# A decoder layer with 32 experts: places of the weight ring, the last transfers in halves, and where the residual is added

## The chip, the cores and the metric

The kernel runs on one core of a Trainium2 chip. The metric is the device time of one execution in microseconds (us); the shown value is the median of three runs.

## The reference

One layer over 256 tokens of 1024 channels, all in fp32:

```
h = rms_norm(x, norm_mix)
x = x + token_mixer(h, ...)        # gated delta rule and mLSTM, 4 heads of 128 each
h = rms_norm(x, norm_ffn)
x = x + moe_ffn(h, ...)            # 32 experts, each token goes to 4 of them
return rms_norm(x, norm_final)

# in moe_ffn, for a token and each of its four experts e
gu   = h @ w_gate_up[e] + b_gate_up[e]            # 1024 -> 2048, gate and up interleaved
gate = min(gu[::2], 7);  up = clip(gu[1::2], -7, 7)
act  = gate * sigmoid(1.702 * gate) * (up + 1)
y    = act @ w_down[e] + b_down[e]                # 1024 -> 1024, weighted with the gate and summed
```

The weights of one expert are 8 MiB of w_gate_up and 4 MiB of w_down; all 32 experts are read, some 400 MB.

## The kernel before, in words

The mixer takes the first 315 us or so. It streams its weights in pieces of 1 MiB through eight half places of a ring in SBUF. The expert part follows and is the subject here.

**Items and groups.** An item is one expert with 64 token slots; a group is two items worked side by side, each on 64 columns of the PE array. There are 16 groups and one lone item (LONE). Group 8 (SHARED) is special: both of its items are the same expert, the one with the most tokens, so it needs one expert's weights for two items.

**The ring.** `ring` has ten places (DOUBLES) of 128 x 4096 fp32, 2 MiB each. An expert's weights are six tiles of that size: four gate/up tiles (GU, parts 0 to 3) and two down tiles (DN, sides 0 and 1). The list `doubles` (line 96 on) gives the order of the 192 transfers, and `released` the order in which PE is done with the tiles. In an ordinary group g both have GU of a, the four DN tiles of group g-1, GU of b. In group 8 `doubles` has the four GU tiles first and the DN tiles of group 7 behind them, while in `released` the DN tiles come first: PE uses the GU tiles twice (gate_up(8, 0) and gate_up(8, 1)) and lets go of them only in the second pass. Transfer i goes to place `ring_order[i % 10]`.

**SyncE (SP)** issues all these transfers on its queue in order. Before transfer i it waits until the tile that lay in this place, `doubles[i - 10]`, is released (`double_done`, line 399), and then calls `fetch` (line 355). `here` (line 300) is what PE waits for: the semaphore of the tile's place.

**PE**, per group n: gate_up(n, 0), down(n-1), gate_up(n, 1), transposes of the activations, scatter(n-1), gather of the rows for group n+1, transposes again. `scatter` (line 877) adds the expert outputs to the sums over all experts, which stay in PSUM banks 0 to 3 (two halves of 512 channels for each 128 tokens); `seed_sums` opens them with the bias of the down projection. At the end (from line 967) come gate_up of the lone item, down(15, side 0), its transposes, a wait for the copies of these by ACT and DVE, eight small products named keep_busy, down(15, side 1), the two sides of the lone item's down with the scatter of group 15 between them, and scatter_lone.

**DVE and ACT** do the clamped SwiGLU between gate_up and down, and the copies out of PSUM. At the end DVE adds the residual (`residual`, line 1381: four adds of 128x512, PSUM plus xs into xs), ACT squares xs and sums each row, DVE and ACT form the reciprocal root, and DVE multiplies xs with it and with norm_final into hn, which SP stores.

Of the kernel before, what the change touches and what calls it, by code (L numbers as in the profile page):

```python
# [20 lines left out]
F32 = mybir.dt.float32  # L21
# [4 lines left out]
ACT = mybir.ActivationFunctionType  # L26
AX = mybir.AxisListType

P = 128
# [5 lines left out]
HALF = 512  # L35
SLOTS = 64
RING = 8
DOUBLES = 10
MIXER_PLACES = 4
PIECE = 2048  # L40
# [3 lines left out]
def decoder_layer(nc, x, norm_mix, w_in, gdn_conv, gdn_a_log, gdn_dt_bias, gdn_norm, ml_conv,  # L44
# [71 lines left out]
    released.extend((DN, col, side) for side in range(2) for col in weights_of(N_GROUPS - 1))  # L116
    doubles.extend((DN, LONE, side) for side in range(2))
    released.extend((DN, LONE, side) for side in range(2))
    place_of = {d: i for i, d in enumerate(doubles)}
    release_of = {d: i for i, d in enumerate(released)}  # L120
    assert len(place_of) == len(release_of) == 6 * E

    with ExitStack() as ctx:
        def sb(name, shape, dt=F32):
# [4 lines left out]
        def sem(name):  # L129
            if name not in sems:  # L130
                sems[name] = ctx.enter_context(nc.semaphore(name))
            return sems[name]
# [120 lines left out]
        place = by_expert(MORE * EXTRA).rearrange("e (r k) -> e r k", r=MORE)  # L253
        placed, shift = by_expert(EXTRA), by_expert(EXTRA)

        bank = [ctx.enter_context(nc.psum_tensor(f"bank{i}", [P, HALF], F32)) for i in range(4)]
        bank45 = ctx.enter_context(nc.psum_tensor("bank45", [P, 2, HALF], F32))
        bank67 = ctx.enter_context(nc.psum_tensor("bank67", [P, 2, HALF], F32))
        B = [b[:, :] for b in bank] + [bank45[:, 0, :], bank45[:, 1, :], bank67[:, 0, :], bank67[:, 1, :]]


        onehot = ltm[:, 0, :, :]
# [21 lines left out]

        def double(d):

            return ring[:, ring_order[place_of[d] % DOUBLES], :]

        def full(place):

            if place < MIXER_PLACES:
                return f"w_full{2 * place}", MOE_FIRST // RING
            return f"ring_full{place}", 0

        def left_here(eng, place, n):

            name, before = full(place)
            eng.wait_ge(sem(name), n * 16 + 16 * (before + len([i for i in range(len(doubles)) if ring_order[i % DOUBLES] == place]) + 1))

        def here(eng, d):  # L300

            name, before = full(ring_order[place_of[d] % DOUBLES])
            eng.wait_ge(sem(name), 16 * (before + place_of[d] // DOUBLES + 1))

        def done_with(eng, d):

# [21 lines left out]
        def by_block(place, k):  # L328
            return place.rearrange("p (k c) -> p k c", k=k)
# [8 lines left out]
        def _(sp):  # L338
# [16 lines left out]
            def fetch(i, e):  # L355
                kind, col, part = doubles[i]
                src = (gu_v, dn_v)[kind][bass.ds(e, 1), :, part, :].rearrange("e p c -> p e c")
                sp.dma_start(by_block(double(doubles[i]), 1), src).then_inc(sem(full(ring_order[i % DOUBLES])[0]), 16)

            def fixed(col):  # L360
                return STAND_IN + 1 + col
# [28 lines left out]
                fetch(i, fixed(doubles[i][1]))  # L390

            expert = {col: fixed(col) for col in range(FIXED)}
            for i in range(DOUBLES, len(doubles)):
                col = doubles[i][1]
                if col not in expert:
                    if len(expert) == FIXED:
                        sp.wait_ge(sem("items_ready"), 1)
                    expert[col] = sp.value_load(ids[0:1, col:col + 1], min_val=0, max_val=E - 1)
                sp.wait_ge(sem("double_done"), release_of[doubles[i - DOUBLES]] + 1)
                fetch(i, expert[col])  # L400

            left = left_count(sp)
            with sp.If(left > 0):
# [73 lines left out]
        def _(pe):  # L477
# [354 lines left out]
            def down(n, sides=(0, 1)):  # L832

                if sides[0] == 0:
                    pe.wait_ge(sem("turned_copied"), n * 2 + 2)
                    pe.wait_ge(sem("xT_ready"), n * 2 + 4)
                for side in sides:
                    of = [(DN, weights_of(n)[min(e, len(weights_of(n)) - 1)], side) for e in range(2)]
                    for d in of:
                        here(pe, d)  # L840
                    for j in range(4):
                        at = j * P + side * SLOTS
                        for half in range(2):
                            for e in range(2):
                                mm = pe.matmul(B[6 + half][e * SLOTS:(e + 1) * SLOTS, :], actT[:, e, at:at + SLOTS],  # L845
                                               by_block(double(of[e]), 4)[:, j, half * HALF:(half + 1) * HALF],
                                               start=(side == 0 and j == 0), stop=(side == 1 and j == 3),
                                               skip_group_check=True)
                                if j == 3 and half == 1 and (e == 1 or of[0] != of[1]):
                                    mm.then_inc(sem("double_done"), 1)  # L850

            def down_lone(side, w):

                for j in range(4):
                    at = j * P + side * SLOTS
                    for half in range(2):
                        mm = pe.matmul(B[4 + half][half * SLOTS:(half + 1) * SLOTS, :], actT_left[:, at:at + SLOTS],  # L857
                                       by_block(w, 4)[:, j, half * HALF:(half + 1) * HALF],
                                       start=(side == 0 and j == 0), stop=(side == 1 and j == 3),
                                       skip_group_check=True)  # L860
                return mm
# [81 lines left out]
            turn_weighted(0, 1)  # L943
            open_gate_up(1, 0)
            turn_act(0, 1, 3)
            for n in range(1, N_GROUPS):
                gate_up(n, 0)
                pe.wait_ge(sem("scat_ready"), n)
                if n == 1:
                    seed_sums()  # L950
                down(n - 1)
                gate_up(n, 1)
                pe.wait_ge(sem("y_copied"), n * 2)
                turn_act(n, 0, 6)
                scatter(n - 1)
                pe.wait_ge(sem("onehot_ready"), n * (2 * T) + 4 * T)
                gather(n + 1, 1)
                pe.wait_ge(sem("turned_copied"), n * 2 + 1)
                gather(n + 1, 0)
                pe.wait_ge(sem("xT_ready"), n * 2 + 3)  # L960
                turn_act(n, 1, 7)
                pe.wait_ge(sem("xT_ready"), n * 2 + 4)
                turn_weighted(n, 6)
                open_gate_up(n + 1, 0)
# [4 lines left out]
            down(last, (0,))  # L969
            turn_act(N_GROUPS, 0, 4)  # L970
            turn_weighted(N_GROUPS, 5)
            pe.wait_ge(sem("turned_copied"), N_GROUPS * 2 + 1)
            pe.wait_ge(sem("scat_ready"), N_GROUPS + 1)
            keep_busy(8, 4)
            down(last, (1,))

            def scatter_lone():
                for t in range(T):
# [5 lines left out]

            for side in range(2):
                d = (DN, LONE, side)
                here(pe, d)
                down_lone(side, double(d)).then_inc(sem("double_done"), 1)
                if side == 0:
                    scatter(last)  # L990
            pe.wait_ge(sem("y_copied"), N_GROUPS * 2 + 2)
# [42 lines left out]
        def _(dve):  # L1034
# [607 lines left out]
                    dve.wait_ge(sem("sums_done"), n * T + 2 * T)  # L1642

            for t in range(T):
                dve.wait_ge(sem("sums_done"), t + 1)
                residual(t, "x3_ready")
            for t in range(T):
                mean_square(2, t)
            for t in range(T):
                dve.wait_ge(sem("root_ready"), 2 * T + t + 1)  # L1650
                link(dve.reciprocal(rstd[:, t:t + 1], rstd[:, t:t + 1]))
                dve.scalar_tensor_tensor(out=hn[:, t, :], in0=xs[:, t, :], scalar=rstd[:, t:t + 1], in1=fnorm[:, :],
                                         op0=ALU.mult, op1=ALU.mult).then_inc(sem("result_ready"), 1)


# [1 line left out]
        def _(se):  # L1657
# [174 lines left out]
            with se.If(left > 0):  # L1832
                with se.Fori(0, left) as n:
                    se.wait_ge(sem("glu_g_ready"), n + ITEMS + 1)
                    se.activation(glu_s, glu_g, ACT.Sigmoid, scale=SWIGLU_ALPHA).then_inc(sem("glu_s_ready"), 1)
                    se.wait_ge(sem("act_turned"), n + ITEMS + 1)
                    se.activation(actT_left, B[6], ACT.Identity).then_inc(sem("turned_copied"), 1)
                    se.wait_ge(sem("double_done"), n * 2 + len(doubles) + 2)
                    se.activation(ysb[0:SLOTS, 0:HALF], B[4][0:SLOTS, :], ACT.Identity).then_inc(sem("y_copied"), 1)
                    se.activation(ysb[SLOTS:P, HALF:D], B[5][SLOTS:P, :], ACT.Identity).then_inc(sem("y_copied"), 1)  # L1840
            se.activation(rstd[:, :], rstd[:, :], ACT.Sqrt).then_inc(sem("root_warmed"), 1)
            for t in range(T):
                se.wait_ge(sem("x3_ready"), t + 1)
                squares(t)
            for t in range(T):
                root(2, t)

# [21 lines left out]
```

## Time and profile before

| what | value |
|---|---|
| median of 3 runs | 1260.62 us (1257.66 to 1260.63) |
| profiled execution | 1257.48 us, its span 1255.5 us |
| PE busy | 1183.1 us, 94% |
| DVE, ACT, POOL busy | 314.8, 129.1, 33.7 us |
| moved by DMA | 441.27 MB, mean 351 GB/s over the span |
| mean granted TensorE clock | 0.985 |

The page divides the span in 40 slices of 31.4 us and gives for each the busy share of every engine and the GB/s of the transfers. A busy share says how much an engine does, not whether it sets the end. For that there are the waits (who waited for whom), the chain that ended last, and the time from the issue of a transfer to its landing, which holds the time in the queue behind earlier transfers too.

### The profile page before, as it was taken

How to read it: one execution, taken by the hardware profiler on the slowest of the kernel's cores; microseconds unless marked ns; L12 is line 12 of the kernel's file. 1: busy time of each engine (PE TensorE's matmuls, PEld its weight loads, DVE VectorE, ACT ScalarE, POOL GpSimd, SP SyncE). 2: the span in 40 equal slices, each digit the busy share in tenths (PEclk: the TensorE clock that was granted, in tenths of full speed). 3: DMA queues.
4: the chain of work that ended last, by engine and by line, in shares of the span. 5: the costliest groups of instructions: out<-in, count | busy, mean ns of one | idle time of the engine just before them, and what ended most of it. 6: DMA issues, size and time to landing. Idle time of an engine off the chain costs nothing.

```text
span 1255.5 us, 13834 instructions
## 1 busy us (share of the span) xinstructions
PE 1183.1 (94%) x5889; PEld 623.5 (50%) x5889; DVE 314.8 (25%) x686; ACT 129.1 (10%) x216; POOL 33.7 (3%) x48
## 2 busy tenths in 40 slices
PE   8999999999999999999899898999999898899986
PEld 6889999985633443434334242434434243434342
DVE  2784325252520211102011110102111010202012
ACT  3551001101000000000000000000000000000001
POOL 3700000000000000000000000000000000000000
PEclk9999999999899999999999999999999999999999
DMA  9933323474699999999999999899999999999993
GB/s 269 328 101 107 105 91 109 176 300 187 253 430 416 428 428 428 427 429 426 427 430 426 428 427 418 360 428 427 429 428 426 428 428 426 429 427 427 429 428 146
DMA packets 61582, 441.27 MB, mean 351 GB/s; under 512 B 8176, under 2 KB 32976, under 8 KB 36848
## 3 DMA queue, kind: packets, MB, share of 16 engines
q1 hardware_dynamic: 57104, 438.38, 85.0%
q10 hardware_dynamic: 4416, 1.99, 0.7%
q8 instruction: 48, 0.79, 0.3%
q14 instruction: 14, 0.11, 0.0%
HBM read 439.30 MB, written 1.05 MB: 351 GB/s over the span
## 4 chain that ended last, share of the span: by engine, by line
PE 65%; DMA 31%; DVE 3%; issue 0%; SPq 0%; ACT 0%; DVEq 0%
DMA ring<-in_w_down 31%; PE bank L805 21%; PE bank L845 14%; PE bank L493 13%; PE bank L509 3%; PE bank L785 3%; PE bank L746 2%; PE bank L882 2%; PE bank L716 1%; PE bank L705 1%; PE bank L797 1%; PE bank L857 1%; PE bank L516 1%; PE bank L579 0%; DVE cvg L1440 0%; PE bank L867 0%
## 5 line engine op out<-in xcount | busy, mean ns | idle before, releaser
L805 PE MATMUL bank<-ring,cvg 128*64 128x512 f32 x2112 | 461.6, 593 | 9.0 <-DMA ring<-in_w_gate_up 8.7
L805 PEld LDWEIGHTS bank<-ring,cvg 128*64 128x64 f32 x2112 | 151.2, 137 | 300.2 <-issue 274.9
L845 PE MATMUL bank<-ring,cvg 128*64 128x512 f32 x1024 | 236.3, 618 | 38.7 <-DMA ring<-in_w_down 38.7
L1450 DVE TENSOR_SCALAR cvm<-bank 128x512 f32<-128x512 f32 x33 | 22.8, 691 | 654.8 <-PE bank L805 654.8
L845 PEld LDWEIGHTS bank<-ring,cvg 128*64 128x64 f32 x1024 | 80.6, 142 | 192.5 <-issue 192.4
L493 PE MATMUL bank<-ring 128*128 128x256 f32 x768 | 171.7, 382 | 0.0
L493 PEld LDWEIGHTS bank<-ring 128*128 128x128 f32 x768 | 145.4, 192 | 19.9 <-issue 0.7
L1801 ACT ACTIVATE cvm<-cvm 128x512 f32<-128x512 f32 x33 | 20.8, 630 | 501.7 <-DVE cvm L1450 501.7
L785 PEld LDWEIGHTS bank<-ltm,hn 128*128 128x128 f32 x544 | 67.8, 199 | 7.1 <-issue 7.1
L785 PE MATMUL bank<-ltm,hn 128*128 128x128 f32 x544 | 67.9, 284 | 0.0
L882 PE MATMUL bank<-vb,ltm 128*128 128x512 f32 x128 | 57.7, 593 | 0.0
L1810 ACT ACTIVATE vb<-bank 128x512 f32<-128x512 f32 x32 | 17.4, 595 | 250.1 <-PE bank L845 250.1
L1440 DVE TENSOR_TENSOR cvg<-bank,ffn_rows 128x512 f32<-128x512 f32 x34 | 23.4, 691 | 66.2 <-PE bank L785 66.2
L882 PEld LDWEIGHTS bank<-vb,ltm 128*128 128x128 f32 x128 | 23.2, 192 | 23.8 <-issue 23.8
L1805 ACT ACTIVATE cvg<-bank 128x512 f32<-128x512 f32 x32 | 18.8, 588 | 99.2 <-PE bank L867 99.2
L746 PE MATMUL bank<-ring 128*128 128x512 f32 x64 | 27.6, 592 | 0.0
L867 PEld LDWEIGHTS bank<-ident,cvg 128*128 128x128 f32 x132 | 18.4, 206 | 13.4 <-issue 13.0
L1455 DVE SCALAR_TENSOR_TENSOR cvm<-cvm 128x512 f32<-128x512 f32 x33 | 22.9, 693 | 3.8 <-DVE cvm L1451 0.5
L1459 DVE TENSOR_TENSOR cvg<-cvm 128x512 f32<-128x512 f32 x33 | 22.8, 692 | 1.1
L867 PE MATMUL bank<-ident,cvg 128*128 128x128 f32 x132 | 22.9, 296 | 0.0
L1451 DVE TENSOR_SCALAR cvm<-bank 128x512 f32<-128x512 f32 x33 | 22.4, 680 | 0.0
L509 PEld LDWEIGHTS bank<-ring 128*128 128x128 f32 x176 | 20.6, 192 | 0.3
(315 smaller groups left out, 615.1 us busy)
## 6 DMA issues: line engine op xcount, KB each, us to landing
ring<-in_w_gate_up SPq DMA_DIRECT2D x128, 2048.0 KB, 34.6
ring<-in_w_down SPq DMA_DIRECT2D x64, 2048.0 KB, 36.7
ring<-in_w_in SPq DMA_DIRECT2D x24, 1024.0 KB, 6.6
ring<-in_w_out SPq DMA_DIRECT2D x4, 1024.0 KB, 5.0
ring<-in_w_up_ml SPq DMA_DIRECT2D x2, 1024.0 KB, 5.1
ring<-in_w_up_gdn SPq DMA_DIRECT2D x2, 1024.0 KB, 5.0
xs<-in_x SPq DMA_DIRECT2D x2, 512.0 KB, 4.6
out<-hn SPq DMA_DIRECT2D x2, 512.0 KB, 2.7
```

The source lines that it names most:

```text
L493: mm = pe.matmul(dst[:, c * S:(c + 1) * S], lhs, rhs, start=(k == 0), stop=(k == KC - 1))
L509: mm = pe.matmul(B[banks[i // 4]][:, (i % 4) * P:(i % 4 + 1) * P], lhs, rhs, start=True, stop=True)
L746: return pe.matmul(B[2 * t + n], gate_g[:, kk, t * P:(t + 1) * P], slot3((OUT_FIRST + i) % RING, 2)[:, k, n * HALF:(n + 1) * HALF], start= ...
L785: mm = pe.matmul(B[6 + b][:, (k % 4) * P:(k % 4 + 1) * P], by_row[:, k // 2, k % 2, :], onehot[:, t, :], start=(t == 0), stop=(t == T - 1))
L805: mm = pe.matmul(B[4 + half][side * SLOTS:(side + 1) * SLOTS, :], xT[:, k, e * SLOTS:(e + 1) * SLOTS], w[:, (k % 2) * PIECE + at:(k % 2) * ...
L845: mm = pe.matmul(B[6 + half][e * SLOTS:(e + 1) * SLOTS, :], actT[:, e, at:at + SLOTS], by_block(double(of[e]), 4)[:, j, half * HALF:(half ...
L867: mm = pe.transpose(B[to][:, c * P:(c + 1) * P], by_row[:, c, :], ident[:, :])
L882: mm = pe.matmul(B[2 * t + half], scat[:, t, :], ysb[:, half * HALF:(half + 1) * HALF], start=False, stop=False, skip_group_check=True)
L1440: dve.tensor_tensor(xT[:, 4 * b:4 * b + 4, :], B[6 + b].rearrange("p (k s) -> p k s", k=4), bc(ffn_rows[:, 4 * b:4 * b + 4].unsqueeze(2), ...
L1450: dve.tensor_scalar(g2, both[:, :, :, 0], SWIGLU_LIMIT, None, ALU.min).then_inc(sem("glu_g_ready"), 1)
L1455: dve.scalar_tensor_tensor(out=glu_u, in0=glu_u, scalar=1.0, in1=glu_g, op0=ALU.add, op1=ALU.mult).then_inc(sem("glu_u_ready"), 1)
L1459: dve.tensor_tensor(act[:, e, :], glu_u, glu_s, ALU.mult).then_inc(sem("act_ready"), 1)
```

## The change

1. *Places.* Transfer i goes to the place of `released[i - 10]` in place of `doubles[i - 10]`, and SP waits for that release. Up to group 8 both orders are the same.
2. *Halves.* The last six transfers, the four down tiles of group 15 and the two of the lone item, go out as two transfers of 1 MiB each with a semaphore for each half. The two tiles of a side alternate: first halves of both, then second halves. PE waits for the half that it needs.
3. *Order at the end.* down(15, side 1) moves ahead of the waits for the copies of the lone item's transposes, and keep_busy(8) goes.
4. *Residual.* In group 4 PE adds x (xs) into the sums by four products with the identity. DVE's adds at the end go. The last norm reads the sums from PSUM: ACT squares from there (into xs), and DVE's last product takes them from there.

```
-    place_of = {d: i for i, d in enumerate(doubles)}
-        bank = [... f"bank{i}", [P, HALF] ... for i in range(4)]
+        sums = [... f"bank{2 * t}{2 * t + 1}", [P, 2, HALF] ... for t in range(T)]

         def double(d):
-            return ring[:, ring_order[place_of[d] % DOUBLES], :]
+            return ring[:, place_at[d], :]
+        HALVED = doubles[-6:]
+        place_at, turn_at, turns = {}, {}, [0] * DOUBLES
+        for i, d in enumerate(doubles):
+            s = ring_order[i] if i < DOUBLES else place_at[released[i - DOUBLES]]
+            place_at[d], turn_at[d] = s, turns[s]
+            turns[s] += 1

+        def half_here(eng, d, half):
+            if half == 0:
+                here(eng, d)
+            else:
+                eng.wait_ge(sem(second_full(d)), 16 * (MOE_FIRST // RING + 1) if HALVED.index(d) < 4 else 16)

-            for i in range(DOUBLES, len(doubles)):
+            for i in range(DOUBLES, len(doubles) - len(HALVED)):
...
-                sp.wait_ge(sem("double_done"), release_of[doubles[i - DOUBLES]] + 1)
+                sp.wait_ge(sem("double_done"), i - DOUBLES + 1)
                 fetch(i, expert[col])
+            def fetch_half(d, half):
+                at = slice(half * PIECE, (half + 1) * PIECE)
+                src = dn_v[bass.ds(expert[d[1]], 1), :, d[2], at].rearrange("e p c -> p e c")
+                sp.dma_start(by_block(double(d)[:, at], 1), src).then_inc(...)
+            for pair in (HALVED[0:2], HALVED[2:4], HALVED[4:5], HALVED[5:6]):
+                sp.wait_ge(sem("double_done"), doubles.index(pair[-1]) - DOUBLES + 1)
+                for half in range(2):
+                    for d in pair:
+                        fetch_half(d, half)

@@ down
-                    for d in of:
-                        here(pe, d)
                     for j in range(4):
+                        for d in of:
+                            if d in HALVED:
+                                half_here(pe, d, j // 2)
+                            elif j == 0:
+                                here(pe, d)

+            def add_residual():
+                for t in range(T):
+                    for half in range(2):
+                        pe.matmul(B[2 * t + half], ident[:, :], xs[:, t, half * HALF:(half + 1) * HALF],
+                                  start=False, stop=False, skip_group_check=True)
             for n in range(1, N_GROUPS):
                 gate_up(n, 0)
...
+                if n == 4:
+                    add_residual()
                 down(n - 1)
@@ end of PE's work
             turn_weighted(N_GROUPS, 5)
+            down(last, (1,))
             pe.wait_ge(sem("turned_copied"), N_GROUPS * 2 + 1)
             pe.wait_ge(sem("scat_ready"), N_GROUPS + 1)
-            keep_busy(8, 4)
-            down(last, (1,))
...
-                here(pe, d)
-                down_lone(side, double(d)).then_inc(sem("double_done"), 1)
+                down_lone(side, double(d), lambda half: half_here(pe, d, half)).then_inc(sem("double_done"), 1)
@@ end of DVE's work
-                dve.wait_ge(sem("sums_done"), t + 1)
-                residual(t, "x3_ready")
...
-                dve.scalar_tensor_tensor(out=hn[:, t, :], in0=xs[:, t, :], scalar=rstd[:, t:t + 1], in1=fnorm[:, :],
+                dve.scalar_tensor_tensor(out=hn[:, t, :]..., in0=sums[t][:, :, :],
+                                         scalar=rstd[:, t:t + 1], in1=fnorm[:, :]...,
@@ end of ACT's work
-                se.wait_ge(sem("x3_ready"), t + 1)
-                squares(t)
+                se.wait_ge(sem("sums_done"), t + 1)
+                se.activation(xs[:, t, :]..., sums[t][:, :, :], ACT.Square,
+                              accum_out=ss[:, t:t + 1]).then_inc(sem("x_squared"), 1)
```

## Rows read from the trace of the kernel before

**Rows 1.** The page, its 40 slices: GB/s of all transfers in each.

```profile
GB/s 269 328 101 107 105 91 109 176 300 187 253 430 416 428 428 428 427 429 426 427 430 426 428 427 418 360 428 427 429 428 426 428 428 426 429 427 427 429 428 146
```

**Rows 2.** Windows: busy per engine (instructions), granted clock, DMA share, GB/s.

```profile
340.00:783.00 443.00, 417.56 (x2016) 169.72 (x2014) 76.77 (x191) 27.06 (x47) 0.00 (x0) 0.99 1.01 427
786.50:789.00 2.50, 2.50 (x14) 1.03 (x12) 0.00 (x0) 0.00 (x0) 0.00 (x0) 1.00 0.00 0
```

**Rows 3.** SyncE's issues from 1182 to 1190 us, and their time to landing.

```profile
L358 SPq DMA_DIRECT2D ring<-in_w_down x3: 332/333/333, 1182.3 to 1189.6; - x3
...
DMA to landing us min/median/max: 42.6/44.0/45.0
```

**Rows 4.** The chain that ended last, from 1166 us: start, us, what.

```profile
1166.31 8.59 PE bank L845 x32
...
1175.53 39.59 DMA ring<-in_w_down
...
1215.25 7.09 PE bank L845 x32
1222.33 0.68 PE bank L867 x4
...
1223.84 2.02 PE bank L524 x16
1225.86 7.02 PE bank L845 x32
1232.88 3.43 PE bank L857 x16
1236.31 3.63 PE bank L882 x8
1239.94 3.61 PE bank L857 x16
```

**Rows 5.** SyncE's issues from 741.5 to 789 us, two, and their time to landing.

```profile
L358 SPq DMA_DIRECT2D ring<-in_w_gate_up x2: 333/685/1037, 742.0 to 788.6; - x2
...
DMA to landing us min/median/max: 9.0/27.0/45.0
```

**Rows 6.** Timeline of PE around group 8: start, us, line, tiles, idle before.

```profile
767.67 7.09 PE L845 MATMUL bank<-ring,cvg 128*64 128x512 f32 x32 [2.44 <-DMA ring<-in_w_down]
777.46 7.09 PE L845 MATMUL bank<-ring,cvg 128*64 128x512 f32 x32 [2.70 <-DMA ring<-in_w_down]
...
784.78 13.93 PE L805 MATMUL bank<-ring,cvg 128*64 128x512 f32 x64
```

**Rows 7.** Time to landing: the issue at 863.3 us, then those from 520 to 560.

```profile
DMA to landing us min/median/max: 22.4/22.4/22.4
...
DMA to landing us min/median/max: 29.1/34.5/42.4
```

**Rows 8.** PE's waits from 784 to 1215 us: total, times, longest.

```profile
PE bank L845 <- DMA ring<-in_w_down: 17.2, 8, 2.7
```

**Rows 9.** Windows of 3.0 and 2.4 us, columns as in rows 2.

```profile
1166.30:1169.30 3.00, 2.99 (x8) 1.11 (x10) 0.00 (x0) 0.00 (x0) 0.00 (x0) 0.50 1.01 431
1212.80:1215.20 2.40, 0.03 (x2) 0.00 (x0) 2.18 (x4) 0.63 (x1) 0.00 (x0) 1.00 0.99 423
```

**Rows 10.** Timeline of DVE and ACT at the end.

```profile
1245.50 2.73 DVE L1386 TENSOR_TENSOR xs<-xs,bank 128x512 f32<-128x512 f32 x4 [1.23 <-PE bank L981]
1245.79 0.21 ACT L1841 ACTIVATE rstd<-rstd 128x8 f32<-128x8 f32 x1
1246.94 1.06 ACT L1664 ACTIVATE hn<-xs 128x1024 f32<-128x1024 f32 x1 [0.94 <-DVE xs L1386]
...
1248.27 1.06 ACT L1664 ACTIVATE hn<-xs 128x1024 f32<-128x1024 f32 x1 [0.17 <-DVE xs L1386]
...
1249.74 1.29 DVE L1652 SCALAR_TENSOR_TENSOR hn<-xs,rstd,fnorm 128x1024 f32<-128x1024 f32 x1
```

**Rows 11.** The page's costliest groups: ACT's copies out of PSUM.

```profile
L1810 ACT ACTIVATE vb<-bank 128x512 f32<-128x512 f32 x32 | 17.4, 595 | 250.1 <-PE bank L845 250.1
```

More of the change, by code:

```diff
@@ L118, in decoder_layer @@
     released.extend((DN, LONE, side) for side in range(2))
-    place_of = {d: i for i, d in enumerate(doubles)}
     release_of = {d: i for i, d in enumerate(released)}
-    assert len(place_of) == len(release_of) == 6 * E
+    assert len(set(doubles)) == len(release_of) == 6 * E
     with ExitStack() as ctx:
@@ L254, in decoder_layer @@
         placed, shift = by_expert(EXTRA), by_expert(EXTRA)
-        bank = [ctx.enter_context(nc.psum_tensor(f"bank{i}", [P, HALF], F32)) for i in range(4)]
+        sums = [ctx.enter_context(nc.psum_tensor(f"bank{2 * t}{2 * t + 1}", [P, 2, HALF], F32)) for t in range(T)]
         bank45 = ctx.enter_context(nc.psum_tensor("bank45", [P, 2, HALF], F32))
         bank67 = ctx.enter_context(nc.psum_tensor("bank67", [P, 2, HALF], F32))
-        B = [b[:, :] for b in bank] + [bank45[:, 0, :], bank45[:, 1, :], bank67[:, 0, :], bank67[:, 1, :]]
+        B = [sums[t][:, n, :] for t in range(T) for n in range(2)] + [bank45[:, 0, :], bank45[:, 1, :], bank67[:, 0, :], bank67[:, 1, :]]
         onehot = ltm[:, 0, :, :]
@@ L293, in full, with second_full @@
             return f"ring_full{place}", 0
+        def second_full(d):
+            i = HALVED.index(d)
+            return f"w_full{2 * i + 1}" if i < 4 else f"lone_full{i - 4}"
+        def half_here(eng, d, half):
[3 more added lines that the diff above has]
+                eng.wait_ge(sem(second_full(d)), 16 * (MOE_FIRST // RING + 1) if HALVED.index(d) < 4 else 16)
         def left_here(eng, place, n):
             name, before = full(place)
-            eng.wait_ge(sem(name), n * 16 + 16 * (before + len([i for i in range(len(doubles)) if ring_order[i % DOUBLES] == place]) + 1))
+            eng.wait_ge(sem(name), n * 16 + 16 * (before + turns[place] + 1))
         def here(eng, d):
-            name, before = full(ring_order[place_of[d] % DOUBLES])
-            eng.wait_ge(sem(name), 16 * (before + place_of[d] // DOUBLES + 1))
+            name, before = full(place_at[d])
+            eng.wait_ge(sem(name), 16 * (before + turn_at[d] + 1))
         def done_with(eng, d):
@@ L357, in fetch @@
                 src = (gu_v, dn_v)[kind][bass.ds(e, 1), :, part, :].rearrange("e p c -> p e c")
-                sp.dma_start(by_block(double(doubles[i]), 1), src).then_inc(sem(full(ring_order[i % DOUBLES])[0]), 16)
+                sp.dma_start(by_block(double(doubles[i]), 1), src).then_inc(sem(full(place_at[doubles[i]])[0]), 16)
             def fixed(col):
@@ L398, in _ @@
                     expert[col] = sp.value_load(ids[0:1, col:col + 1], min_val=0, max_val=E - 1)
[L399 removed]
+                sp.wait_ge(sem("double_done"), i - DOUBLES + 1)
                 fetch(i, expert[col])
+            def fetch_half(d, half):
+                at = slice(half * PIECE, (half + 1) * PIECE)
+                src = dn_v[bass.ds(expert[d[1]], 1), :, d[2], at].rearrange("e p c -> p e c")
+                sp.dma_start(by_block(double(d)[:, at], 1), src).then_inc(sem(second_full(d) if half else full(place_at[d])[0]), 16)
+            for pair in (HALVED[0:2], HALVED[2:4], HALVED[4:5], HALVED[5:6]):
[3 more added lines that the diff above has]
+                        fetch_half(d, half)
             left = left_count(sp)
@@ L850, in down, with down_lone @@
                                     mm.then_inc(sem("double_done"), 1)
-            def down_lone(side, w):
+            def down_lone(side, w, wait=None):
                 for j in range(4):
+                    if wait and j % 2 == 0:
+                        wait(j // 2)
                     at = j * P + side * SLOTS
@@ L1651, in _ @@
                 link(dve.reciprocal(rstd[:, t:t + 1], rstd[:, t:t + 1]))
-                dve.scalar_tensor_tensor(out=hn[:, t, :], in0=xs[:, t, :], scalar=rstd[:, t:t + 1], in1=fnorm[:, :],
+                dve.scalar_tensor_tensor(out=hn[:, t, :].rearrange("p (n c) -> p n c", n=2), in0=sums[t][:, :, :],
+                                         scalar=rstd[:, t:t + 1], in1=fnorm[:, :].rearrange("p (n c) -> p n c", n=2),
                                          op0=ALU.mult, op1=ALU.mult).then_inc(sem("result_ready"), 1)
@@ L1840, in _ @@
                     se.activation(ysb[SLOTS:P, HALF:D], B[5][SLOTS:P, :], ACT.Identity).then_inc(sem("y_copied"), 1)
+                    se.wait_ge(sem("sums_done"), n * T + 2 * T)
             se.activation(rstd[:, :], rstd[:, :], ACT.Sqrt).then_inc(sem("root_warmed"), 1)
             for t in range(T):
-                se.wait_ge(sem("x3_ready"), t + 1)
-                squares(t)
+                se.wait_ge(sem("sums_done"), t + 1)
+                se.activation(xs[:, t, :].rearrange("p (n c) -> p n c", n=2), sums[t][:, :, :], ACT.Square,
+                              accum_out=ss[:, t:t + 1]).then_inc(sem("x_squared"), 1)
             for t in range(T):
```

1 line of the change is left out of this document (removed).

## The prediction

> **What bounds the kernel now.** The page comes first: its 40 slices say which stretch has which limit. From slice 14 on the transfers move 426 to 430 GB/s, slice after slice, with dips in slices 25 and 26 alone (418, 360) until the last one [rows 1]. A stretch by itself confirms it: from 340 to 783 us the 16 DMA engines are busy 1.01 of the time at 427 GB/s [rows 2]. So the expert weights, 192 transfers of 2 MiB, set the pace. The chain of waits looks different, 65% PE, but its long DMA links (39.59 us for one transfer) are the time in the queue behind others, not the work of one.
>
> Two places are left where the transfers don't set the pace. One is the hole: at 786.5 to 789.0 us not one byte moves, with PE fully busy [rows 2]. The other is the end: the last three issues at 1182.3, 1185.8 and 1189.6 us land 42.6, 44.0 and 45.0 us later [rows 3], at 1224.9, 1229.8 and 1234.6 us, hence 4.9 us a transfer; yet PE goes on to 1243.55 us [rows 4], 8.9 us after the last byte.
>
> **Part 1, the place released next.** The hole, exactly: the transfer issued at 742.0 us lands 45.0 us later, at 787.0; the next one is issued only at 788.6 us and lands after 9.0 us, at 797.6 [rows 5]. Two landings in a row are 10.6 us apart instead of 4.9, so the hole costs 10.6 - 4.9 = 5.7 us. Why so late: in group 8 both items use one expert's weights, so the order of release is down(7)'s four tiles, then the four gate/up tiles, while the order of transfer is the other way round. The transfer at 788.6 takes the place of the first gate/up tile, which PE lets go of 3.5 us into the stretch at 784.78. The four down tiles had been free since 767.67 + 7.09 = 774.8 and 777.46 + 7.09 = 784.6 us [rows 6]. With the change the first two of the waiting transfers go out at 774.8 and the next two at 784.6, before the 742.0 transfer lands at 787.0, and 4 x 4.9 us of queued work reaches to 806.6; the gate/up places come free from 788.3 on. The hole closes whole: -5.7 us on every later landing.
>
> Would a later hole open, as PE stays where it is while transfers run ahead? The tightest issue after it is at 863.3 us, the first one after PE's long gather and transpose work; it waits 22.4 us in the queue [rows 7], and would wait 16.7. A transfer into an empty queue took 9.0 [rows 5], so 7.7 us are spare. Can PE use the earlier data? From 784 to 1215 us it waits 17.2 us in 8 waits for down weights alone [rows 8], more than 5.7, so it comes to the end 5.7 us earlier.
>
> **Part 2, the end.** Halves first. gate_up of the lone item ends at 1212.8 us (PE's idle stretch begins there [rows 9]), and PE waits until 1215.25 for the second tile of side 0. All times shift by -5.7: end of gate_up 1207.1. The pair comes as a0, b0, a1, b1, so the two first halves are in when formerly the first tile was: the second tile's 1215.1 less 4.9 is 1210.2, less 5.7 is 1204.5. PE starts at once, and the second halves (1209.4) are in before it needs them at 1210.7: side 0 runs 1207.1 to 1214.2. The two transposes (0.91 us from 1222.33 to 1223.24, the 0.68 of it in [rows 4]) end at 1215.1. Before, PE now waited for the DVE copy (0.6) and ran eight keep_busy products (2.02 [rows 4]); the change goes straight into side 1, and the copies by ACT and DVE lie beside it. Its first halves are in at 1224.9 - 4.9 - 5.7 = 1214.3; half of 7.06 us takes it to 1218.6; the second halves land at 1219.2, a wait of 0.6; end 1222.8. Lone side 0 (3.43; its second half is in at 1224.1 and needed at 1224.5), scatter (3.63), lone side 1 (3.61) [rows 4] end at 1233.5; the last half lands at 1234.6 - 5.7 = 1228.9 and is needed at 1231.7. So PE, not the transfers, still ends last: 1243.55 - 1233.5 = 10.0 us gained, 5.7 of them by part 1 and 4.3 here (2.4 for the wait of side 0, 2.6 for copy and keep_busy, less the new 0.6 and rounding).
>
> What halves cost: rows of 8 KB instead of 16 KB, six more issues, and a pair that waits for its later release (3.4 us). The last is hidden under 42 us of queue. For the rate nothing in the trace shows 8 KB rows: no loss at one end; at the other the mixer's pieces in 1 KB rows, 328 GB/s in slice 2 [rows 1], would stretch 12 MiB from 29.4 to 38 us. I take 0.3 us, near the 16 KB rate, and since PE has 2.8 us in hand at the last half, it costs nothing. At 328 GB/s the last half would land at 1237.5, PE end at 1239.3, and 5.8 of the gain be gone.
>
> **Part 3, the residual.** Four products of ident with xs, 128x512, fp32, in group 4. The scatter has four of that shape: 3.63 us [rows 4]. They lie at about 537 us, where transfers issued between 520 and 560 us wait at least 29.1 us in the queue [rows 7], so releases 3.6 us later starve nothing, and PE then waits for DMA in every group. Nothing at the end; 3.6 us if PE were the bound. Off the end go DVE's four adds (2.73 us, of which the first square waits for two and the second for all [rows 10]). ACT's first square began at 1246.94, its second at 1248.27. Now the sums of t = 0 are ready at 1245.5, but ACT is busy with the warming root until 1246.0 [rows 10]: that is late next. The squares run 1246.0 and 1247.2, end 1248.35 instead of 1249.4: -1.05. Reading PSUM: ACT took 595 ns for 512 elements from it [rows 11] against 1.06 us for 1024 from SBUF, so one square is 1.02 to 1.19; I take 1.06. DVE's adds from PSUM are 0.68 for 512, the last product from SBUF 1.29 for 1024: 1.29 to 1.37, I take 1.29. Together this may take back 0.4.
>
> **Sum.** -5.7 - 4.3 - 1.05 = -11.0 us. The profiled execution took 1257.48 us (span 1255.5): 1246.5. It lies 3.1 us under the median of the three timed runs, 1260.62; these stand at two levels, 1257.66 and twice 1260.6, for a reason that the profile doesn't show. Shifted, the levels are 1246.6 and 1249.6. I take 1248.
>
> **A rule against halves.** A lone transfer took 9.0 us, a queued one 4.9 [rows 3, 5]: 4.1 us of each are hidden by the queue. The Trainium skill ("DMA: Bandwidth & Descriptors", section Bandwidth) gives a 1 MB transfer alone 6.15 us, 341 GB/s, and asks for 1 MiB at least; an estimate by that page, twelve in a row, is 73.8 us against 29.4, and the time would be 1248 + 44.4 - 2.8 = 1290. That is the first rival below, at its dearest; the spacing of 4.9 in a full queue speaks for overlap, so no such cost stands in my sum.
>
> **Rivals.**
> - *Halves pay their start.* If the 4.1 us were not hidden for small transfers, six more would put the last landing at 1228.9 + 24.6 = 1253.5, PE's end 1.8 later, and the kernel at 1248 + 21.8 = 1270: slower. It decides from 2.3 us each on. Against: about 90 transfers in a row at 4.9. Chance 0.02.
> - *The hole moves.* PE is behind after group 8; if transfers starve once more, the 5.7 us are lost and parts 2 and 3 remain. From 1212.8 on: side 0 to 1219.9, transposes 1220.8, side 1 to 1228.4 (second half 1224.9), the rest 10.7: 1239.1, -4.4 and -1.05: 1253.6. The 7.7 us to spare speak against. 0.06.
> - *Clock.* After a wait of 2.7 us at 1166.3 the granted clock was 0.50 for 3 us (1.2 GHz), and 32 products took 8.59 instead of 7.09 [rows 4, 9]; after 2.4 us at 1212.8 it stayed 1.00. The change has no keep_busy and one wait of 0.6: a drop costs 1.5, 1249.5. For the whole chain at half clock, 26 us more would make 1274; nothing so long is seen. 0.05, the first price nearly all of it.
> - *The residual doesn't shorten the end* (ACT's root or slow PSUM reads take it back): 1249. 0.07.
>
> **Chances.** The forecast has 0.80 with its own range of 1245 to 1251. About 0.3% (3.8 us) is what a measurement of this kernel tells from no change. Faster by more than that hold the forecast, the clock, the residual case and most of the moved hole: 0.94; within: 0.03 (part of the moved hole, slow 8 KB rows with both levels against me); slower: 0.03. The range takes in both levels, the slow rate in part and the moved hole's near end: 1244.5 to 1253.
>
> **What would show it.** No slice under 425 GB/s between 340 us and the last megabytes; issues at about 775 and 785 us; last landing about 1229; PE in one piece from 1193 to 1233 but for 0.6 us; no L524 rows there; squares straight after the warming root; end of span about 1244.5. Wrong if a zero-byte stretch stands elsewhere, if the halves land over 3 us apart, or if PE waits for the last half.

## The result, and the profile after

The changed kernel took 1250.47 us (median of 5 runs, 1248.82 to 1254.91) against 1260.63 for the kernel before beside it: a ratio of 0.9926 with a 95% interval of 0.9905 to 0.9947, or -9.3 us (-12.0 to -6.7). A second comparison gave 0.9921 (0.9907 to 0.9935), -10.0 us.

First a line of the page of the profile after: GB/s in its 40 slices. Against [rows 1] the dips of slices 25 and 26 are gone (428, 426).

```profile
GB/s 257 309 101 134 101 102 101 101 301 203 224 432 417 428 428 427 429 427 427 428 427 427 429 427 428 426 428 427 428 427 428 428 427 428 429 428 427 428 422 203
```

Then windows of the profile after; columns as in [rows 2]: busy per engine, granted clock, DMA share, GB/s. The first row is a stretch of the mixer, the second the one in which not a byte moved before, the last three the end.

```profile
50.00:100.00 50.00, 50.00 (x223) 42.54 (x223) 41.04 (x59) 23.96 (x35) 4.68 (x2) 0.90 0.45 139
786.50:789.00 2.50, 2.50 (x14) 1.04 (x12) 0.00 (x0) 0.00 (x0) 0.00 (x0) 1.00 0.99 419
...
1226.00:1230.00 4.00, 2.83 (x16) 1.15 (x16) 0.00 (x0) 0.00 (x0) 0.00 (x0) 1.00 0.99 414
1230.00:1234.00 4.00, 4.00 (x22) 1.46 (x18) 0.00 (x0) 1.09 (x2) 0.00 (x0) 1.00 0.62 260
1234.00:1237.10 3.10, 3.10 (x9) 1.31 (x8) 0.00 (x0) 0.00 (x0) 0.00 (x0) 1.00 0.29 122
```

SyncE's timeline after around group 8: two of the waiting transfers go out with the first release of down tiles, two with the second, as forecast (this profile runs 6 us late, so 780.9 and 790.7 in place of 775 and 785).

```profile
780.91 0.85 SPq L376 DMA_DIRECT2D ring<-in_w_gate_up  x2
790.70 0.85 SPq L376 DMA_DIRECT2D ring<-in_w_down  x2
794.61 10.63 SPq L376 DMA_DIRECT2D ring<-in_w_gate_up  x4
```

Time to landing after, first of the issue at 336.3 us, then of the last two, at 1207.0 and 1211.2 us. The first landing of the steady stretch is at 336.3 + 7.6 = 343.9 us, the last at 1211.2 + 25.8 = 1237.0.

```profile
DMA to landing us min/median/max: 7.6/7.6/7.6
...
L423 SPq DMA_DIRECT2D ring<-in_w_down x2: 1981/3028/4075, 1207.0 to 1211.2; - x2
...
DMA to landing us min/median/max: 25.8/26.7/27.6
```

PE's timeline after, from the lone item's gate_up on: it answers to [rows 4]. Start, us, line, tiles, idle before.

```profile
1200.92 13.90 PE L834 MATMUL bank<-ring,cvg 128*64 128x512 f32 x64
1214.65 7.03 PE L877 MATMUL bank<-ring,cvg 128*64 128x512 f32 x32
...
1222.52 3.65 PE L877 MATMUL bank<-ring,cvg 128*64 128x512 f32 x16
...
1227.34 3.65 PE L877 MATMUL bank<-ring,cvg 128*64 128x512 f32 x16 [1.17 <-DMA ring<-in_w_down]
1230.80 3.63 PE L891 MATMUL bank<-ring,cvg 128*64 128x512 f32 x16
...
1234.36 3.70 PE L916 MATMUL bank<-vb,ltm 128*128 128x512 f32 x8
1237.99 3.65 PE L891 MATMUL bank<-ring,cvg 128*64 128x512 f32 x16
...
1242.44 1.99 PE L1023 MATMUL bank<-vb,ltm 64*128 64x512 f32 x8 [0.80 <-DVE vb L1644]
```

Side 0 (1214.65) starts without a wait, side 1 (1222.52) right behind the transposes, with one wait of 1.17 us for its second halves. PE's last product on weights ends at 1241.67 us, 4.6 us after the last landing, where it was 8.9. The tail, ACT and DVE after, to be read beside [rows 10]:

```profile
1243.91 0.21 ACT L1881 ACTIVATE rstd<-rstd 128x8 f32<-128x8 f32 x1
1244.02 1.01 ACT L1884 ACTIVATE xs<-bank 128x1024 f32<-128x1024 f32 x1
...
1245.02 1.01 ACT L1884 ACTIVATE xs<-bank 128x1024 f32<-128x1024 f32 x1
...
1246.45 1.28 DVE L1690 SCALAR_TENSOR_TENSOR hn<-bank,rstd,fnorm 128x1024 f32<-128x1024 f32 x1
```

**A table without the mixer.** The execution profiled after is a late one (1254.19 us): its first landing of the steady stretch is 6.0 us later than before, in a stretch that the change does not touch. So every kernel is read from its first landing on. "Last" is the last landing, "PE" the end of PE's products on weights, both counted from that first landing, in us of one profiled execution each; "tail" is from PE's end to the end of the span; the ratio is that of the timed runs to the kernel before. "Changed, again" and the variants are described under the experiments.

```
kernel                first   last     PE    tail   ratio (95%)
before                337.9   896.8  905.7   12.0
changed               343.9   893.2  897.8   10.5   0.9926 (0.9905 to 0.9947)
changed, again        338.8   893.3  897.9   10.5   0.9921 (0.9907 to 0.9935)
places alone          338.0   892.4  901.4   11.9   0.9954 (0.9940 to 0.9969)
end alone             339.2   897.4  901.9   11.9   0.9961 (0.9947 to 0.9974)
residual alone        339.6   898.4  909.1   10.5   0.9991 (0.9980 to 1.0003)
whole last tiles      340.8   893.0  901.1   10.6   0.9933 (0.9910 to 0.9957)
old order             340.1   893.0  898.9   10.5   0.9921 (0.9899 to 0.9943)
residual late         337.5   893.0  901.0   10.5   0.9937 (0.9916 to 0.9959)
all in halves         339.7   905.6  910.2   10.5   1.0023 (1.0009 to 1.0037)
with a pause          343.0   903.2  907.7   10.5   0.9993 (0.9978 to 1.0008)
root early            339.7   892.9  897.5   11.9   0.9927 (0.9912 to 0.9942)
root between          339.7   892.5  897.2    9.7   0.9918 (0.9900 to 0.9936)
```

From its first landing to the end of the span the changed kernel is 9.3 us shorter than the kernel before (-3.6 to the last landing, -4.3 from there to PE's end, -1.4 in the tail).

### The profile page after: what moved, and what is told of

The parts are those of the page before. It is cut to its first block, busy times and chain, and to the rows that moved or that the text cites. A ratio compares the mean times of both kernels' runs of the same rounds, so it can differ in the third digit from the quotient of the medians.

```text
span 1252.2 us, 13838 instructions
## 1 busy us (share of the span) xinstructions
PE 1187.1 (95%) x5881; PEld 626.7 (50%) x5881; DVE 311.2 (25%) x682; ACT 129.1 (10%) x216; POOL 33.6 (3%) x48
## 3 DMA queue, kind: packets, MB, share of 16 engines
HBM read 439.30 MB, written 1.05 MB: 352 GB/s over the span
## 4 chain that ended last, share of the span: by engine, by line
PE 65%; DMA 30%; SPq 2%; DVE 2%; issue 0%; ACT 0%; ACTq 0%; DVEq 0%
DMA ring<-in_w_down 30%; PE bank L834 21%; PE bank L522 14%; PE bank L877 13%; PE bank L538 3%; PE bank L814 2%; PE bank L775 2%; PE bank L916 2%; SPq L423 2%; PE bank L745 1%; PE bank L734 1%; PE bank L826 1%; PE bank L891 1%; PE bank L545 1%; PE bank L553 0%; PE bank L608 0%
## 5 line engine op out<-in xcount | busy, mean ns | idle before, releaser
L877 PE MATMUL bank<-ring,cvg 128*64 128x512 f32 x1024 | 233.1, 611 | 31.2 <-DMA ring<-in_w_down 31.2
L522 PE MATMUL bank<-ring 128*128 128x256 f32 x768 | 176.4, 390 | 0.0
L522 PEld LDWEIGHTS bank<-ring 128*128 128x128 f32 x768 | 148.9, 196 | 21.4 <-issue 1.0
L901 PEld LDWEIGHTS bank<-ident,cvg 128*128 128x128 f32 x132 | 18.4, 207 | 13.4 <-issue 13.0
L1492 DVE TENSOR_SCALAR cvm<-bank 128x512 f32<-128x512 f32 x33 | 22.4, 680 | 0.0
L1821 ACT ACTIVATE ring<-bank 128x512 f32<-128x512 f32 x14 | 8.4, 597 | 121.5 <-PE bank L522 121.5
```

The lines of the kernel that those rows point to most:

```text
L522: mm = pe.matmul(dst[:, c * S:(c + 1) * S], lhs, rhs, start=(k == 0), stop=(k == KC - 1))
L901: mm = pe.transpose(B[to][:, c * P:(c + 1) * P], by_row[:, c, :], ident[:, :])
```

## The experiments

**Each part alone.** The three parts, each put into the kernel before by itself.

```
# places alone: s = place_at[released[i - DOUBLES]], wait for double_done >= i - 9
# end alone: halves of the last six, down(last, (1,)) ahead of the waits, no keep_busy
# residual alone: add_residual() in group 4, last norm from PSUM
```

> The kernel before with the new places alone (whole transfers, old order at the end, residual on DVE). The forecast's part 1 says -5.7 us: no zero-byte stretch near 787 us, issues at about 775 and 785 us, landings from there on 5.7 us earlier, time 1254.9. A second theory, from the profile after (where the landings from 344 us on came only 3.6 us earlier than before and the transfers' last microseconds were spread over 7 us instead of 3.5): the pause had let a lagging DMA engine catch up, and without it the lag grows, so only 3 to 4.5 us are left: 1256 to 1257.5. If the hole only moved: no change, 1260.6.

Measured: 0.9954, -5.8 us (-7.6 to -3.9). In the profile the last landing comes 4.4 us earlier and PE's end 4.3. The forecast's 5.7 lies inside the interval of the timed runs, but the table speaks for less, as the second theory does: the eight profiles with the new places and neither a pause nor all tiles in halves stand at 892.4 to 893.3, the three with the old places at 896.8 to 898.4. Pair by pair that is 3.5 to 6.0 us, 4.8 on average, a little above the theory's 3 to 4.5. The windows of this kernel show the hole closed:

```profile
786.50:789.00 2.50, 2.50 (x15) 0.97 (x12) 0.00 (x0) 0.00 (x0) 0.00 (x0) 1.00 1.02 429
```

> The kernel before with the last six transfers in halves and the new order at the end, alone. The forecast's part 2 says -4.3 us: 1256.3, hole at 787 us still there, PE's end 4.3 us earlier against the last landing (4.6 us after it instead of 8.9). If halves pay their start: slower. If the clock falls without keep_busy: about 1258. The DMA lag at the end stays at 3 to 4 us, as the pause is still there.

Measured: 0.9961, -4.9 us (-6.7 to -3.3). The hole stays: issues at 743.3 and 789.9 us, landing after 45.0 and 8.7. PE ends 4.6 us after the last landing (1241.11 against 1236.54) in place of 8.9: -4.3, the forecast. Counted from the first landing PE's end is 3.8 us earlier (901.9 against 905.7), since the last landing of this profile is 0.6 us later.

```profile
L376 SPq DMA_DIRECT2D ring<-in_w_gate_up x2: 332/682/1031, 743.3 to 789.9; - x2
...
DMA to landing us min/median/max: 8.7/26.9/45.0
```

> The kernel before with the residual added by PE in group 4 and the last norm read from PSUM, alone. The forecast's part 3 says -1.05 us; the profile after says -1.4 (PE's end to the end of the span 10.5 instead of 11.95 us): 1259.2 to 1259.6, the residual's four products hidden. If they are not hidden: +2.2.

Measured: 0.9991 (0.9980 to 1.0003), -1.1 us, not told from zero by timing. Only the tail of the profile shows it: 10.5 instead of 12.0 us. PE's end in this profile is 3.4 us late for two reasons that its rows show. The last landing is 1.6 us later; the gap between two landings at the hole is 10.9 us here, 10.5 before. And after a wait of 2.43 us, up to 1218.7, the granted clock fell to 0.50 (1.2 GHz) from 1219.3 to 1222.7, which is a mean of 0.62 over the window below: side 0 of down(15) took 8.78 us for the 7.09 of [rows 4], in the very place where the kernel before waited 2.4 us without a drop [rows 9]. First PE's row, then the window of that stretch:

```profile
1218.68 8.78 PE L869 MATMUL bank<-ring,cvg 128*64 128x512 f32 x32 [2.43 <-DMA ring<-in_w_down]
```

```profile
1218.60:1221.60 3.00, 2.92 (x10) 1.09 (x12) 0.52 (x1) 0.00 (x0) 0.00 (x0) 0.62 1.01 431
```

The sum of the three, -11.8 us, is more than the whole's -9.3 or -10.0, a difference that their intervals allow.

**Inside part 2.** Halves and order apart, each undone in the changed kernel: the last six tiles fetched whole, or

```
+            keep_busy(8, 4)
-            down(last, (1,))      # ahead of the two waits
+            down(last, (1,))      # behind them
```

> The changed kernel with the last six transfers whole. From the profile after: side 0 would start when its second tile is whole (1217.0 instead of 1214.7), side 1 end at 1234.0 instead of 1231.0, the rest follow: +3.0 us, less 0.36 for the rows of 16 KB, so 1253.1 against 1250.5. If halves bring nothing (PE would be the bound anyway): 0.

Measured: PE's end 901.1 instead of 897.8, +3.3; timed 0.9933, between 0.9 and 1.5 us above the two ratios of the changed kernel, which the intervals can't tell apart. The waits that the halves took away are back, 2.43 us before side 0 and 1.81 before side 1:

```profile
1214.36 7.09 PE L869 MATMUL bank<-ring,cvg 128*64 128x512 f32 x32 [2.43 <-DMA ring<-in_w_down]
...
1224.15 7.09 PE L869 MATMUL bank<-ring,cvg 128*64 128x512 f32 x32 [1.81 <-DMA ring<-in_w_down]
```

> The changed kernel with the old order at the end: waits for the copies and keep_busy(8) before down(15, side 1). In the profile after PE waits 1.2 us for the second halves of side 1; the 2.6 us put back push side 1's first half to 1225.1 and its end from 1231.0 to 1232.2: +1.2 us (less than the 2.6 it holds). If the products held the clock up, it would be faster or the same, and the granted clock in the last 30 us higher than in the changed kernel.

Measured: PE's end 898.9, +1.1, as expected; timed 0.9921, the same as the changed kernel. The copy and keep_busy fill 1.2 us of waiting for side 1, and keep no clock up that falls without them: the granted clock of the changed kernel is 1.00 from 1200 to 1244 us, over the place where they stood (about 1222 to 1225) too.

**Where the residual is added.**

```
-                if n == 4:
-                    add_residual()
+            add_residual()        # behind down(last, (1,)) and the two waits
```

> The changed kernel with add_residual at the end of PE's work (behind down(15, side 1)) instead of group 4. PE is the bound there: +3.4 us, the whole price of the four products, which measures what group 4 hides. If they are free everywhere: 0.

Measured: PE's end 901.0, +3.2 us, timed 0.9937 (+1.4 to +2.0, which the intervals can't tell from nothing). This is the price that group 4 hides: with the products there the last landing is 893.2 or 893.3, without them 893.0. PE has room for them, since in the changed kernel it stands waiting for down weights 31.2 us in all.

```profile
PE bank L877 <- DMA ring<-in_w_down: 31.2, 15, 2.9
```

**All tiles in halves.** Each expert tile in two transfers of 1 MiB:

```
+                for half in range(2):
+                    at = slice(half * PIECE, (half + 1) * PIECE)
+                    sp.dma_start(by_block(double(doubles[i])[:, at], 1),
+                                 src[:, :, at]).then_inc(sem(full(place_at[doubles[i]])[0]), 16)
...
```

> The changed kernel with every expert tile fetched in two transfers of 1 MiB (rows of 8 KB), PE waiting for both. In the profile after the last 12 halves land 2.48 us apart instead of 4.89 / 2 = 2.445, so 0.07 us a tile: 186 tiles more give +13 us, less what PE-bound stretches hide. If the 0.07 is no property of the row length: 0. If each transfer pays its 4.1 us of start: several hundred us.

Measured: 1.0023, 1262.5 us, 12.2 us over the changed kernel of the first comparison by the ratios; the last landing 12.4 us later. The whole steady stretch moves at a lower rate, first this kernel's window, then the changed kernel's:

```profile
400.00:700.00 300.00, 285.23 (x1380) 117.56 (x1378) 50.52 (x122) 18.85 (x33) 0.00 (x0) 0.99 1.01 421
```

```profile
400.00:700.00 300.00, 289.11 (x1400) 118.44 (x1398) 50.44 (x122) 19.93 (x35) 0.00 (x0) 0.99 1.01 428
```

So halves cost 1.6% of the rate, and a start of 4.1 us each is out: it would have been 760 us. The 16 DMA engines are as busy in both (1.01), so they don't starve. Whether the loss comes from the shorter rows (8 KB in place of 16) or from the doubled number of transfers is not separated: both change at once. Six tiles in halves cost 0.4 us by this rate (in the changed kernel the twelve halves land within 29.7 us, where six whole tiles take 29.4); so halving can pay only at the end.

**The missing microsecond of part 1.** A pause in the changed kernel:

```
-                sp.wait_ge(sem("double_done"), i - DOUBLES + 1)
+                sp.wait_ge(sem("double_done"), i if doubles[i] == (GU, 25, 0) else i - DOUBLES + 1)
```

> The changed kernel with one pause put in: the transfer of expert 25's first gate/up tile (about 1010 us) waits until PE has released every tile before it, so the transfers run dry once. The gap between two landings should be about 12 to 14 us instead of 4.9, a hole of 8 to 9 us. Theory of the lag: the spread between the first and the last of the 16 parts of a transfer falls from about 6 to 2 us at the pause, as at 787 us in the kernel before, so the last landing comes later than in the changed kernel by 3 to 4 us less than the hole, and the spread at the end is 3 to 4 us instead of 6.9. Rival: the smaller gain of part 1 has nothing to do with a lag; the last landing comes later by the whole hole and the spread at the end stays near 7.

Measured: the gap between two landings is 15.3 us, so the hole is 10.4 us, and the last landing is 10.0 us later (903.2 - 893.2); timed 0.9993, 8 to 9 us over the changed kernel. Of the expectation one half held. A landing is the last of the 16 increments that a transfer's 16 parts make to its semaphore; the spread is the time from the first of them to the last. The spread does fall: at the end all 16 engines are busy nearly to the last microsecond, where the changed kernel's DMA share decays over 7 us (the last two of its windows above). Windows of this kernel, the dry stretch and the end:

```profile
1048.20:1056.00 7.80, 7.52 (x36) 2.94 (x36) 0.00 (x0) 0.55 (x2) 0.00 (x0) 1.00 0.00 0
...
1239.00:1243.00 4.00, 4.00 (x22) 1.50 (x18) 0.00 (x0) 1.09 (x2) 0.00 (x0) 1.00 1.02 426
1243.00:1246.20 3.20, 3.20 (x11) 1.36 (x8) 0.00 (x0) 0.00 (x0) 0.00 (x0) 1.00 0.44 184
```

But it gave nothing back, in place of 3 to 4 us: from the landing behind the pause to the last one it took 182.7 us, 182.5 and 182.8 in the two profiles of the changed kernel without a pause; the 0.4 between 10.4 and 10.0 arose ahead of the pause. The expectation was wrong in its arithmetic: the gap was taken between landings, a landing is that of the last part, and so the gap already leaves out what the late part catches up. The increments show it: at the pause the first parts of two transfers in a row are 20.3 us apart, the last parts 15.3, and the spread falls from 6.0 to 1.0. What a pause can give back is only lag that grows less afterwards, and here it grew 0.9 us from there to the end, against 1.1 to 1.3 in the changed kernel.

**The last norm.** Two tries to shorten the tail further.

```
# root early: the warming root, and with it the table load, ahead of the lone item's last copy
# root between:
+                se.wait_ge(sem("x_squared"), 2 * T + t + 1)
+                se.activation(rstd[:, t:t + 1], ss[:, t:t + 1], ACT.Sqrt, scale=1.0 / D, bias=NORM_EPS)
# inside the loop over the two squares, and DVE's mean_square steps go
```

> The changed kernel, with the warming root and its table load moved from the very end to ACT's idle time before the lone item's last copy. In the profile after, the first square starts at 1244.02, right behind the warming root, while its sums were there at 1243.6: -0.4 to -0.5 us against the changed kernel, in the profile between PE's end and the first square. If the copy that lies between needs another table, two more loads of 1.3 us come and it is slower by about 1.3.

Measured: 0.9927 (0.9912 to 0.9942), the changed kernel's ratio, and a tail of 11.9 us instead of 10.5. The copy is not what brings the loads back: they stand before the first square and before the roots, behind the branch that asks whether experts are left over. That the branch is what brings them back is likely by their place, but no run tests it. ACT's timeline of this kernel:

```profile
1237.26 0.59 ACT L1869 ACTIVATE vb<-bank 64x512 f32<-64x512 f32 x1 [8.04 <-PE bank L891]
1238.18 1.28 ACT L1884 ACT_TABLE_LOAD   x1 [0.33 <-issue]
1239.48 1.02 ACT L1884 ACTIVATE xs<-bank 128x1024 f32<-128x1024 f32 x1
...
1241.61 1.28 ACT L1708 ACT_TABLE_LOAD   x1
```

> The changed kernel with the root of the first 128 tokens taken between the two squares, and scale and epsilon inside the root (DVE's two small steps go). In the profile after, DVE's first product starts at 1246.45, when both squares are done; here it should start 0.75 us earlier against PE's end and the span's end follow: -0.7 to -0.8 us, most of it visible only in the profile. If DVE's products then stretch beside ACT's square (both read PSUM): less than 0.3.

Measured: 0.9918 (0.9900 to 0.9936), against 0.9921 for the changed kernel on the same chip; the tail is 9.7 us instead of 10.5, -0.8. It is the fastest kernel of the study by its profile, by less than timing can show. DVE's first product now runs beside ACT's second square, and both keep their length:

```profile
1240.29 0.20 ACT L1885 ACTIVATE rstd<-ss 128x1 f32<-128x1 f32 x1
1240.40 1.00 ACT L1882 ACTIVATE xs<-bank 128x1024 f32<-128x1024 f32 x1
...
1240.72 1.28 DVE L1688 SCALAR_TENSOR_TENSOR hn<-bank,rstd,fnorm 128x1024 f32<-128x1024 f32 x1
```

**Once more.**

> The changed kernel once more, beside the kernel before on the same chip: 0.991 to 0.993 of it. From the first landing of the steady stretch (about 340 us) to the last landing 893.1 us as in every run with the new places, against 896.8 to 898.4 with the old ones, and a spread of 6.7 to 7.0 us at the end; if these were accidents of one run, other values.

Measured: 0.9921, 893.3 us to the last landing and a spread of 6.8 us at the end. The values of the first profile are no accident of one run.

## Why the prediction was right, and where its terms were off

The time is inside the range and on the forecast side; 1250.47 is 2.5 us above the 1248 that was given, and the change is -9.3 or -10.0 us where -11.0 was forecast. The mechanisms held; the sizes of two terms were off in opposite directions, part 1 too large by 2.1 us in the first pair of profiles and part 3 too small by 0.4. By its steps:

- *Part 1, -5.7: mechanism right, term too large.* The hole closed as said, at the releases named, and no other one opened: the tight issue, at 863.3 us before, waited 18.4 us in the queue after (16.7 forecast). But the last landing came 3.6 us earlier in the first pair of profiles, and on average 4.8 (892.6 over eight profiles, with 0.4 taken off where the last six are halved, against 897.4 over three). The forecast took the gap between two landings for the loss and let all later landings move by it. (The issue at 863.3 us was not quite the tightest either: the one at 800.5, which refills the queue behind the hole, waited 21.5 us against 22.4; it is part of the hole and went with it.)

  The stretch behind the hole did not stay the same. From the landing after it to the last one the three kernels with a hole took 437.1, 437.6 and 438.4 us (0.4 taken off where halves are used), seven of the eight without one 438.6 to 438.7 (the eighth, root between, 437.6, after a step of 1.0 us at the place of the hole). The increments of each transfer's 16 parts say where the difference lies. The first part takes 435.4 to 435.9 us over this stretch (with the same 0.4 taken off) in all eleven profiles, hole or not; what differs is how much further the last part falls behind it. That growth was 1.3, 1.7 and 2.9 us in the kernel before, end alone and residual alone, 2.0 in root between, and 2.8 to 3.2 in the seven others. So part 1 is worth the gap less this lag, 0.3 to 1.6 us a run. That the lag accounts for the missing microsecond is shown by these sums; why it grows, and why it grew less behind two of the three holes, is open.
- *Part 2, -4.3: right, to 0.1.* 8.9 us from the last landing to PE's end became 4.6. The halves' price was taken as 0.3 and is 0.4, and it delays the last landing itself, so counted from the first landing the gain is a little less (3.8 in end alone). Single waits came out a little differently: 1.2 us for side 1's second halves in place of 0.6. The rival in which halves pay their start is refuted by the kernel that fetches all tiles so: 421 GB/s in a full queue. The 341 GB/s that the Trainium skill ("DMA: Bandwidth & Descriptors", section Bandwidth) gives for one 1 MB transfer is not what 1 MiB transfers reach when some ten stand in the queue (an estimate: 25.7 us in the median from issue to landing, at 2.5 us each). The recorded estimate of 73.8 us for twelve used the duration in that row; an estimate by its rate is 36.9, and the twelve of the changed kernel took 29.7.
- *Part 3, -1.05: the term was -1.4 in the profiles* (the timed runs of residual alone can't tell it from nothing). ACT's square from PSUM takes 1.01 us, less than the 1.06 from SBUF and the bound of 1.02; the second starts 1.00 behind the first, in place of 1.33 [rows 10]; and DVE's product from PSUM takes 1.28, where that from SBUF took 1.29. ACT's warming root was indeed what came late next.
- *The residual's products at nothing: right*, and their price where nothing hides it is 3.2 us (3.6 was named).
- *The clock.* No drop in the changed kernel's end. The risk lay with the kernel before: in residual alone a drop after its wait of 2.4 us cost 1.7 us, and halves remove the wait. That is one execution of one kernel; how often it happens no run here tells.
- *The level.* The forecast took a middle of two levels of the timed runs, 1.6 us under 1260.62 - 11.0 = 1249.6. They are not two but a band, and both kernels have it (below). Against the median of the kernel before the forecast would have missed by 0.9 us, so most of the 2.5 us is this choice.

## What to carry to other kernels

When a ring's places are reused in the order of transfer but released in another, compare the two lists: the transfer that stands behind a late release costs a hole, and giving it the place released next cost nothing here. Halve only the last transfers, where PE waits for a first half and the smaller transfers cost a few tenths: that took 3.3 us off PE's end in the profile, while halving all cost 12 us. Price a hole by the last landing of all, not by the gap beside it, and read a pair of profiles from the first instruction that the change can touch.

## What the runs showed of the hardware that was not expected

- *Part of the band of times goes with the granted clock in the mixer.* The five runs of the changed kernel took 1248.82, 1250.47, 1250.15, 1254.19 and 1254.91 us at a mean granted clock of 0.987, 0.986, 0.984, 0.982 and 0.980. In the profile after, the clock was 0.90 from 50 to 100 us, where the kernel before had 0.97; PE is busy the whole 50 us in both. Up to 345 us the clock was at 0.50 (1.2 GHz) for 23.9 us in that profile and for 10.2 in the kernel before, and the first landing is 6.0 us later. In all the profiles 10.2 to 13.7 us at 0.50 go with a first landing at 337.5 to 340.1, 17.1 us with 340.8 and 343.0. Ten runs of the kernel with places alone go from 1251.97 us at 0.989 to 1258.63 at 0.978. It is not the whole band: twenty runs of the kernel before, 1257.7 to 1263.1 us on the same chip, show no such order (1257.75 at 0.982, 1263.14 at 0.984).
- *A transfer's 16 parts drift apart.* With 4.89 us between most landings, the spread between a transfer's first and last part in the changed kernel is 1.7 us at 360 us, 3.7 at 780, 5.4 at 1000 and 6.9 at the end. In the kernel before it falls from 4.0 to 2.1 at the hole and ends at 3.5; with the pause it ends at 1.9.
- *Issues of 1 MiB hold SyncE longer.* An issue of a 2 MiB tile takes 0.33 us in all but three of the 173 from 345 us on in the changed kernel. With all tiles in halves 80 of the issues, the row below, took 2.0 us in the median, and ten of the last twelve of the changed kernel took 2.0 to 5.7. It starved no transfer here: with all tiles in halves every landing of an issue after 800 us came at least 15.3 us after it, in the changed kernel's end at least 25.8. Why an issue takes so long is open.

```profile
L378 SPq DMA_DIRECT2D ring<-in_w_gate_up x80: 1339/1996/3692, 911.3 to 1189.0; - x80
```
